# Heads in pairs over both halves of the array in two attentions, and an earlier load and a deeper drive in an S5 stage

## The reference

```
ffn0, s5, ffn1, ffn2, moba, ffn3      (first half: SwiGLU, S5 state space, SwiGLU x2, attention 1, SwiGLU)
ab, mlp0, mla, mlp1                   (second half: attention 2, relu^2 MLP, attention 3, relu^2 MLP)

# ab: 16 heads of dimension 64, on tiles of 128 queries
gqa:      p = softmax(q @ k.T / 8);            o = p @ v      (8 heads, 2 key heads)
dilated:  p = softmax(q @ k.T / 8 + bias);     o = p @ v      (8 heads, bias per head and distance)
# mla: 16 heads, q and k of dimension 96 (64 + 32 rotated), v of dimension 64
mla:      p = softmax(q @ k.T / sqrt(96));     o = p @ v
mix = concat(o) @ w_out

# s5: u = h @ w_in; per group a linear recurrence over the tokens, x' = lam * x + B u, y = C x + D u
g = gelu(y); g = g * sigmoid(g @ w_glu); out = g @ w_out
```

## Time and profile before

| | us |
|---|---|
| median of 3 runs (lowest to highest) | 1608.7 (1602.38 to 1620.78) |
| the profiled execution, its time | 1601.97 |
| its span on the core | 1600.2 |
| PE busy | 1535.4 (96%) |
| DVE busy | 1015.0 (63%) |
| ACT busy | 768.5 (48%) |
| POOL busy | 414.8 (26%) |

### The profile page before, as it was taken

How to read it: one execution, slowest core, us unless ns; L and a number is a source line. 1 busy time by engine, 2 the same in 40 slices (tenths; PEclk the granted TensorE clock), 3 DMA queues, 4 the chain that set the end, 5 groups by cost and what they waited for, 6 DMA issues and landing times.

```text
span 1600.2 us, 31973 instructions
## 1 busy us (share of the span) xinstructions
PE 1535.4 (96%) x13406; PEld 1476.9 (92%) x13406; DVE 1015.0 (63%) x998; ACT 768.5 (48%) x1007; POOL 414.8 (26%) x392
## 2 busy tenths in 40 slices
PE   9999985999999999999899999999999988999997
PEld 8999985999999999999799999967999987699997
DVE  7767768575566756575575567446766675476665
ACT  6444531454444544476554435655434356553433
POOL 2999925010002000057320001754000033410000
PEclk9999997999999999999999999999999998999999
DMA  7555553445454555545155554431555541145552
GB/s 270 188 207 183 207 114 112 167 171 209 182 208 171 216 201 183 195 168 180 73 185 203 192 186 182 168 110 64 200 185 183 209 160 52 41 183 200 183 208 79
DMA packets 54822, 271.20 MB, mean 169 GB/s; under 512 B 17680, under 2 KB 22032, under 8 KB 23344
## 3 DMA queue, kind: packets, MB, share of 16 engines
q1 hardware_dynamic: 53648, 266.58, 46.6%
q0 software_dynamic: 1088, 3.38, 0.7%
HBM read 266.52 MB, written 3.42 MB: 169 GB/s over the span
## 4 chain that ended last, share of the span: by engine, by line
PE 84%; DVE 7%; ACT 2%; POOL 2%; issue 2%; DMA 1%; SPq 1%; DVEq 0%; POOLq 0%; ACTq 0%
PE ps L658 78%; PE ps L994 2%; PE ps L984 2%; DVE xlo L1526 2%; DVE wlo L1520 1%; PE ps L972 1%; DVE h L1542 1%; DMA uP<-turned_u 1%; ACT whi L1135 1%; ACT pm L1397 0%; POOL pm L523 0%; DVE ps L1739 0%; PE ps L930 0%; POOL rinv L522 0%; POOL sq L467 0%
## 5 line engine op out<-in xcount | busy, mean ns | idle before, releaser
L1520 DVE TENSOR_TENSOR wlo<-raw,whi 128x2048 fp32r<-128x2048 f32 x245 | 572.2, 2338 | 230.3 <-ACT whi L1135 230.0
L1135 ACT CAST whi<-raw 128x2048 fp32r<-128x2048 f32 x245 | 468.4, 1913 | 253.4 <-PE ps L658 241.2
L658 PE MATMUL ps<-xhi,whi 128*128 128x256 f32 x2048 | 570.4, 279 | 7.1 <-DVE xlo L1526 4.1
L658 PE MATMUL ps<-xlo,whi 128*128 128x256 f32 x2048 | 567.6, 277 | 0.0
L658 PE MATMUL ps<-xhi,wlo 128*128 128x256 f32 x2048 | 567.5, 277 | 0.0
L658 PEld LDWEIGHTS ps<-xhi,whi 128*128 128x128 f32 x2048 | 386.3, 189 | 10.7 <-DVE xlo L1526 3.2
L658 PEld LDWEIGHTS ps<-xlo,whi 128*128 128x128 f32 x2048 | 386.3, 189 | 0.0
L658 PEld LDWEIGHTS ps<-xhi,wlo 128*128 128x128 f32 x2048 | 386.2, 189 | 0.0
L658 PE MATMUL ps<-hhi,whi 128*128 128x256 f32 x1216 | 335.7, 276 | 0.0
L658 PE MATMUL ps<-hlo,whi 128*128 128x256 f32 x1216 | 335.6, 276 | 0.0
L658 PE MATMUL ps<-hhi,wlo 128*128 128x256 f32 x1216 | 335.6, 276 | 0.0
(11 more groups left out here) (244 smaller groups left out, 1935.6 us busy)
## 6 DMA issues: line engine op xcount, KB each, us to landing
raw<-in_wstream SPq DMA_DIRECT2D x245, 1024.0 KB, 4.8
raw<-in_wstream SPq DMA_DIRECT2D x4, 512.0 KB, 7.3
h<-in_xT SPq DMA_DIRECT2D x4, 256.0 KB, 5.8
turned_u<-sq SPq DMA_DIRECT2D x8, 128.0 KB, 4.6
uP<-turned_u SPq DMA_DIRECT2D x8, 128.0 KB, 3.3
turned_y<-gs SPq DMA_DIRECT2D x8, 128.0 KB, 2.1
sq<-turned_y SPq DMA_DIRECT2D x16, 64.0 KB, 2.4
biasA<-bias_rows POOLq DMA_DIRECT2D x5, 192.0 KB, 5.2
```

Of the source, the lines that this page charges most:

```text
L658: return pe.matmul(o, l, r, start=first, stop=last, skip_group_check=True)
L1135: act.copy(whi[:, slot, :], raw[:, slot, :]).then_inc(S("whi_ready"), 1)
L1520: dve.tensor_tensor(wlo[:, slot, :], raw[:, slot, :], whi[:, slot, :], ALU.subtract)\
```

## The change

ab and mla get a version of the attention of their own, `attention_pairs`, with `normalise_pairs` on POOL. moba keeps the old one.

- The unit is a pair p of heads 2p and 2p+1. `scores(p)` alternates between the two heads, with four banks (0, 1, 6, 7) in place of two. `pv(p)` alternates between them as well, with the results in the two halves of one bank.
- `pm` and `pT` have four buffers. The two new ones of each lie over `tk` and `tsq`, which the attention doesn't need.
- PE has the scores of four heads ahead: scores(0), scores(1), then for each p `scores(p+2), turn(2p), pv(p-1), turn(2p+1)`. PE starts on the output projection with three k of each half at the last two pairs.
- The transposes of odd heads without a bias are copied by DVE, the rest by ACT. DVE's order in a pair is: maxima of two heads (2p+4, 2p+5), the copy of head 2p+1, `ylo` of pair p-1.
- POOL makes `rinv` for both heads of a pair at once, when the exponentials of both are done.
- ACT and DVE split chunk FO+1 of mla at pair 3 in place of the last heads.
- S5: `load_u(1)` comes ahead of `load_k`. PE runs `drive(2)` after the last input product and then drive(j+3) in place of drive(j+2) ahead of read_out(j).

The core of the diff:

```diff
             store_u(1)
+            load_u(1)
             load_k()
             one(F5 + 6)
-            load_u(1)
             one(F5 + 7)
...
+            def normalise_pairs(st):
+                for p in range(KT):
+                    b = slice(2 * (p % 2), 2 * (p % 2) + 2)
+                    pool.wait_ge(S(st + "_exp"), 4 * p + 4)
+                    chain(pool.tensor_tensor(rinv[:, b, :], rs[:, b, :],
+                                             power[:, 1:2].unsqueeze(2).to_broadcast([P, 2, TT]), ALU.pow))
+                    for s in (2 * p, 2 * p + 1):
+                        x = pm4[s % 4]
+                        pool.tensor_tensor(x[:, :, :], x[:, :, :],
+                                           rinv[:, s % 4, :].unsqueeze(2).to_broadcast([P, TT, T]), ALU.mult)\
+                            .then_inc(S(st + "_pn"), 1)
...
+                drive(2)
                 for j in range(KT):
-                    if j + 2 < KT:
-                        drive(j + 2)
+                    if j + 3 < KT:
+                        drive(j + 3)
                     read_out(j)
...
+                def scores(p):
+                    if p >= 2:
+                        pe.wait_ge(S(st + "_exp"), 4 * (p - 1))
+                    for t in range(TT):
+                        for s in (2 * p, 2 * p + 1):
+                            last = pe.matmul(ps[:, SCORE_BANKS[s % 4], t * T:(t + 1) * T],
+                                             hs[s]["q"][:, t * P:(t + 1) * P], hs[s]["k"][:, 0:T],
+                                             start=True, stop=True, skip_group_check=True)
...
+                def pv(p):
+                    pe.wait_ge(S(st + "_ptc_even"), p + 1)
+                    pe.wait_ge(S(st + "_ptc_odd"), p + 1)
...
+                    for kt in range(TT):
+                        for s in (2 * p, 2 * p + 1):
+                            hd = hs[s]
+                            last = pe.matmul(ps[hd["row"]:hd["row"] + 64, 4 + p % 2, 0:T],
+                                             vtok[:, kt, hd["v"]:hd["v"] + 64], pT4[s % 4][:, kt, :],
+                                             start=kt == 0, stop=kt == TT - 1, skip_group_check=True)
...
+                for p in range(KT):
+                    if p + 2 < KT:
+                        scores(p + 2)
+                    turn(2 * p)
+                    if p >= 1:
+                        pv(p - 1)
+                    turn(2 * p + 1)
+                    if p == KT - 2:
+                        chunk_ready(FO, None)
+                        out_part(0, 0, 3)
+                    if p == KT - 1:
+                        out_part(1, 0, 3)
+                pv(KT - 1)
```

ACT's order in `attention_pairs`:

```diff
+                for p in range(KT):
+                    turned(2 * p)
+                    if p + 2 < KT:
+                        exponents(2 * p + 4)
+                    if p >= 1:
+                        out_high(p - 1)
+                    if hs[2 * p + 1]["bias"] is not None:
+                        turned(2 * p + 1)
+                    if p + 2 < KT:
+                        exponents(2 * p + 5)
```

And DVE's:

```diff
+                for p in range(KT):
+                    if p + 2 < KT:
+                        maxima(2 * p + 4)
+                        maxima(2 * p + 5)
+                    if hs[2 * p + 1]["bias"] is None:
+                        turned_odd(2 * p + 1)
+                    if p >= 1:
+                        out_low(p - 1)
+                    if st == "mla" and p == 3:
+                        split_lo(F + len(TOK[st]) + 4)
```

More of the change, by code:

```diff
@@ L1859, in attention @@
-                    if st == "mla" and s == n:
-                        split_lo(F + len(TOK[st]) + 4)
+                        if s == 0:
+                            dve.wait_ge(S("mask_loaded"), 16)
+                        for t in range(TT):
+                            w = n_keys(hd, t)
+                            dve.scalar_tensor_tensor(out=lg[b][:, t, 0:w], in0=ps[:, b, t * T:t * T + w],
+                                                     scalar=hd["scale"], in1=mask[:, t, 0:w], op0=ALU.mult, op1=ALU.add)\
+                                .then_inc(S(st + "_lg"), 1)
@@ L1861, in attention @@
+                        dve.wait_ge(S(st + "_lg"), 2 * s + 2)
+                        for t in range(TT):
+                            chain(dve.reduce_max(mx[:, b, t:t + 1], lg[b][:, t, 0:n_keys(hd, t)], AX.X))
+                        dve.tensor_scalar(nmx[:, b, :], mx[:, b, :], -1.0, None, ALU.mult).then_inc(S(st + "_nmx"), 1)
                     if 0 <= s - 3 < n and hs[s - 3]["row"] + hs[s - 3]["dv"] == P:
```

189 lines of the change are left out of this document (134 added, 55 removed).

## The result

| | before | after |
|---|---|---|
| median, 20 runs each (lowest to highest), us | 1606.82 (1600.67 to 1620.78) | 1597.65 (1591.76 to 1602.53) |
| the profiled execution, its time, us | 1601.97 | 1598.15 |

The ratio is 0.9932, with a 95% interval of 0.9917 to 0.9947: 0.7% faster, some 9 to 11 us, where 25 were forecast. The median was to be 1584 and is 1597.65; the profiled execution was to take 1577.0 and took 1598.15. The direction was right and the size was not.

A forecast was written before the change was run, and what follows sets the result against it. PE was taken to bound the steady states of ab and mla. Gains of 12.6 + 11.8 + 1 = 25.4 us, taken as 25, from the median 1608.7 gave about 1584, range 1573 to 1600.

The forecast's parts named there:

- the sum: Whole kernel: gains of 12.6 in ab, 11.8 in mla and 1 in S5, taken as 25 us off 1602.0: 1577.0.
- The signs of being wrong: Wrong if PE's clock mid-ab is under 0.9, a pair's records are 0.25 us apart, or S5 moves over 3 us.
- Rival 1: Pairs don't overlap in PE's array: ab gains 6 us, mla 7, with S5 14, so 1595; 12%.
- Rival 2: PE's clock falls in ab: ab gains 0 us, mla 12, with S5 13, so 1596; 14%.
- Do pairs overlap: ab's scores and both stages' `p @ v` run two at a time on PE: 8 records in 1.0 us.
- PE's sum for a pair: PE's work for a pair of heads: ab 3.2 us for 5.3 before, mla 4.0 for 5.0.
- ab: Attention ab: DVE-bound pairs of 5.0, 5.0, 4.4, 4.4 us; last `p @ v` ends at 1089.3; gain 12.6 us.
- mla: Attention mla: pairs of 4.0 us, tail of 9.9, last `p @ v` ends at 1380.7; gain 11.8 us.
- The term "+1": In mla, the split at pair 3 costs DVE and ACT about 2 us each with 1 to spare: +1 us.
- S5: PE's 5.74 us wait before S5's loop goes, y chain begins 2 us later: gain 1 us, bounds -3 and +3.
- Rival 3: Slower: PE at half clock in mla too, 14 us lost there, S5 3 lost; 18 in all, 1627; 4%.
- Rival 4: Better: `nmx` never waits (2.4 us), clock rises earlier in both starts (3), S5 gives 3: gain 33, 1576; 10%.

The follow-up runs named there:

- the tiny matmuls in both kernels: One tiny bf16 matmul of zeros added in each of six ffn and mlp stages: kernel after 1580.83 us, kernel before 1605.28 us.
- experiments 8 and 12: 8: kernel after plus six tiny matmuls, mla's split at the last pair, 1576.91 us; 12: the same with S5 as before the change, 1578.21 us.
- experiment 9: Kernel after plus six tiny matmuls, mla's split at the last pair; ab's odd heads' scores use the even head's q and k: 1580.96 us, 0.9822.
- the two with ACT's copies: Kernel after, late mla split, more tiny matmuls, ACT copying transposes of ab's heads 5 and 7: 1573.04 us; one ffn0 tiny matmul moved: 1574.24 us.
- experiment 3: Kernel after with 123 more tiny matmuls, one in each chunk going through `proj` into banks 4 to 7: 1616.38 us, 1.0047.

## Why the prediction was right in its mechanism and wrong in its size

- **The step that failed is the sum**: "1602.0 - 25 = 1577.0". It gave every other stage its old time, on the strength of "78% of the span are the weight products of line 658, which the change leaves alone". The code of these products was left alone and their pace wasn't: 6.4 and 6.6 us in mlp0 and mlp1 in every profile of the kernel after, and 6.4 to 6.8 more in two of three, in ffn1 or ffn2. 1598.15 - 19.4 = 1578.8 is within 2 us of the forecast 1577.0. With the tiny matmuls in both kernels the distance is 24.5 us for 25, or 23 without ffn0's part. That the interval takes these 19 us is shown; why the pairs bring the long one to mlp0 and mlp1 is open. No rival had this, because I read the before kernel's pace as a constant. The three executions that I had of it spread over 18 us (1602.38 to 1620.78), nearly three times 6.4, and the profiled one (1601.97), faster than all three, had no long stage. That was a hint which I passed over.
- **The signs of being wrong didn't catch it**: the clock in ab, the distance of a pair's records and the S5 stage all came out as they should. All signs lay in the stages that the change touches.
- **Where the time fell is luck**: 1597.65 is inside the wide range of 1573 to 1600, which was made for rivals 1 and 2 (1595 and 1596). It lies beside them by another mechanism.
- **Do pairs overlap**: right. 1.06 us for eight records (1.0 forecast); on one half they take 1.92.
- **PE's sum for a pair**: 3.25 (3.2 forecast) in ab, 3.77 (4.0) in mla.
- **ab**: 13.3 us (12.6 forecast). DVE is the bound with a bias, and its copy costs what was put down: without it 1.5 us come back in the pairs, and 1.3 more in the end of ab. DVE's pairs were 4.63, 4.94 and 4.33 us for 5.0, 5.0 and 4.4. `nmx` waited in three of eight times and added 2.2 us in sum, for the 2.4 put down. The prediction's "3 us longer in sum" for an `nmx` that always waits is wrong by its own terms: 8 x (1.04 - 0.3) is 5.9. The last `p @ v` ended 37.8 us after the first scores (1055.87 to 1093.63) for 39, and after 38.5 and 39.8 in the other two profiles.
- **mla**: 8.0 us in the first pair of profiles (11.8 forecast), and up to 11.6 in others. From the first scores to the last `p @ v` it takes 42.5, 39.0 and 38.0 us in the three profiles, for 38.2 by the forecast's sum. So the total was met where the clock didn't fall behind the split. The term "+1" for the split at pair 3 was mis-sized all the same: 3 us, and 5 where the clock falls. In those two executions it was hidden, because the part ahead of the last scores was 4 to 5 us shorter than forecast (24.3 and 23.3 us, for 28.3). And the tail, 9.9 by the forecast, is 11.6 even with the late split. Not the 2 us of work decided, but what stood behind it: DVE waited for ACT, and both maxima, POOL's products and DVE's copy came late, so that PE paused 1.96 us. I had looked at room in DVE's sum, not at its queue.
- **S5**: PE's wait ahead of the loop went and turn_y(0) kept its place (255.02 for 255.56) where I had it 2 us later; a new wait of 6.74 us for `uP` stands inside the loop. In time nothing can be told: ratio 0.9989 alone, and 1.3 us between experiments 8 and 12, inside their intervals. The 1 us forecast fits, and so would nothing.
- **Rival 1** (no overlap) is out by experiment 9. **Rival 2** (clock falls in ab) is out: 1.00 in pairs with a bias, with PE busy 3.07 of 5.00 us. **Rival 3** is out: mla's pairs ran at 1.00. Half clock came behind the split (0.76 over 14 us), in some executions only. **Rival 4** needed a gain that no run shows.

## What to carry to other kernels

Count the instructions in a window of the stages that a change doesn't touch, and take their pace as something the change can move: a busy share of 100% at full clock hid 4%. Take more than one profile of a kernel before you put a stage's loss down to the change: mla fell short of the forecast by 3.8 us in one profile and by 0.2 in another. Where executions of one kernel spread in steps of the same size, look for a stage with two paces before you add up a forecast. When work is moved into a steady state, follow what is queued behind it on its engine, not only whether the engine has time left. Of the variants here the two with ACT's copies are the fastest, and beat both kernels: 0.9767 (0.9752 to 0.9783) and 0.9799 (0.9774 to 0.9824) of before.

## What the hardware showed that I had not expected

- Weight products of 256 columns ran at 113.3 or 117.8 ns from start to start, with the clock at 1.00 in both. The level held through a stage of more than 1,300 matmuls, and changed behind a wait, a float32 matmul or other work. One change in mid-run was seen, with none of these near (mlp1 without `settle`).
- A tiny bf16 matmul between them can bring the short level back. It costs 0.33 us and saved some 6 us a stage here. It was followed by the long level three products behind a wait (2 of 2). Behind the pair attention only the second one worked in eight kernels, and in experiment 3 only the third behind `settle`, in ffn1 and ffn2 too.
- The same pause of PE, 1.96 us behind the split in mla, was followed by half clock in five of the eight profiles that have it (0.76 on average over the 14 us behind it), and by the full clock in three.
- Two heads on different halves of the array ran side by side whether their matmuls alternated or not (1.06 and 1.07 us for eight records).
- `nmx` on 128x2 took 0.17 us alone and up to 1.02 beside POOL's product (1.00 in the earlier trace rows already). DVE's split beside POOL did the reverse: two products took 4.09 us for 2.04. Both engines can be the one that waits.
